# The shift of the router's token rows taken into TensorE as a product of depth 1

## The reference, cut to what matters

```python
h = rms_norm(x, g_ffn) * (1 + scale2) + shift2      # scale2, shift2: one row for context, one for latent tokens
def moe_swiglu(h, w_router, w_gu, w_down):
    t = h.reshape(B * L, D)
    logits = (t @ w_router).astype(jnp.float32)
    top_v, top_i = lax.top_k(logits, TOP_K)
    top_w = jax.nn.softmax(top_v, axis=-1)
    ...                                             # each expert: silu(t @ gate) * (t @ up) @ down, weighted and summed
```

## Time and profile before

| | |
|---|---|
| time, median of 3 executions | 1950.79 us (1949.42 to 1951.01) |
| the profiled execution, its own time | 1948.53 us |
| its span | 1946.7 us |
| PE busy | 1887.4 us (97%) |
| DVE, ACT, POOL busy | 1118.3, 799.6, 139.3 us |

### The profile page before, as it was taken

How to read it: one execution, slowest core, us unless ns; L and a number is a source line. 1 busy time by engine, 2 the same in 40 slices (tenths; PEclk the granted TensorE clock), 3 DMA queues, 4 the chain that set the end, 5 groups by cost and what they waited for, 6 DMA issues and landing times.

```text
span 1946.7 us, 30525 instructions
## 1 busy us (share of the span) xinstructions
PE 1887.4 (97%) x12501; PEld 1726.0 (89%) x12501; DVE 1118.3 (57%) x1796; ACT 799.6 (41%) x1334; POOL 139.3 (7%) x109
## 2 busy tenths in 40 slices
PE   7999989999999999999998899899999999999998
PEld 6999767999999999999997587889898988989896
DVE  2644776544432444447347853667676766768577
ACT  4221264322211222223213643556565655656564
POOL 2000000200000000110000012220000000002211
PEclk8999999999999999999999999999999999999999
DMA  9425100324231432315271031677677676768762
GB/s 353 162 105 217 55 1 23 109 98 183 77 120 44 168 127 74 119 34 195 92 211 34 1 66 61 149 239 243 224 246 226 214 237 203 248 200 304 255 200 76
DMA packets 94068, 291.55 MB, mean 150 GB/s; under 512 B 15348, under 2 KB 23924, under 8 KB 93920
## 3 DMA queue, kind: packets, MB, share of 16 engines
q1 hardware_dynamic: 86784, 271.20, 42.3%
q0 software_dynamic: 7136, 18.30, 2.9%
HBM read 283.02 MB, written 12.28 MB: 152 GB/s over the span
## 4 chain that ended last, share of the span: by engine, by line
PE 90%; DVE 5%; ACT 1%; DMA 1%; issue 1%; SPq 0%; POOL 0%; POOLq 0%; ACTq 0%; DVEq 0%
PE ps L740 47%; PE ps L1119 12%; PE ps L1108 12%; PE ps L1109 6%; PE ps L806 2%; PE ps L935 2%; PE ps L1112 2%; PE ps L881 1%; DVE pr L2037 1%; DVE nbias L2020 1%; PE ps L1111 1%; PE ps L1204 1%; DMA ada_raw<-ada_w 1%; PE ps L942 1%; ACT pT L1448 0%
## 5 line engine op out<-in xcount | busy, mean ns | idle before, releaser
L1867 DVE TENSOR_TENSOR w_lo<-raw,w_hi 128x1024 fp32r<-128x1024 f32 x394 | 482.1, 1225 | 386.0 <-ACT w_hi L1319 377.4
L1319 ACT ACTIVATE w_hi<-raw 128x1024 fp32r<-128x1024 f32 x394 | 414.5, 1053 | 341.7 <-PE ps L740 171.2
L1108 PE MATMUL ps<-hg,w_hi 128*128 128x416 f32 x1232 | 379.2, 365 | 1.0 <-DVE hg L2311 0.8
L740 PE MATMUL ps<-a_hi,w_hi 128*128 128x320 f32 x1472 | 341.9, 313 | 3.4 <-DVE a_lo L1898 3.4
L740 PE MATMUL ps<-a_hi,w_lo 128*128 128x320 f32 x1472 | 336.7, 310 | 0.0
L740 PE MATMUL ps<-a_lo,w_hi 128*128 128x320 f32 x1472 | 333.8, 308 | 0.0
L1109 PE MATMUL ps<-hg,w_lo 128*128 128x208 f32 x1232 | 319.2, 259 | 0.0
L740 PEld LDWEIGHTS ps<-a_hi,w_hi 128*128 128x128 f32 x1472 | 247.4, 188 | 12.1 <-issue 8.1
L740 PEld LDWEIGHTS ps<-a_lo,w_hi 128*128 128x128 f32 x1472 | 248.6, 189 | 0.0
L740 PEld LDWEIGHTS ps<-a_hi,w_lo 128*128 128x128 f32 x1472 | 245.2, 188 | 0.0
L1109 PEld LDWEIGHTS ps<-hg,w_lo 128*128 128x128 f32 x1232 | 234.7, 191 | 0.4
(11 more groups left out here) (285 smaller groups left out, 2446.5 us busy)
## 6 DMA issues: line engine op xcount, KB each, us to landing
raw<-gu_w SPq DMA_DIRECT2D x220, 512.0 KB, 4.4
raw<-moe_down_w SPq DMA_DIRECT2D x88, 512.0 KB, 4.2
ada_raw<-ada_w SPq DMA_DIRECT2D x21, 2048.0 KB, 8.3
raw<-in_w SPq DMA_DIRECT2D x48, 512.0 KB, 9.8
raw<-down_w SPq DMA_DIRECT2D x22, 512.0 KB, 3.4
raw<-out_w SPq DMA_DIRECT2D x16, 512.0 KB, 3.5
ada_pro<-ada_w SPq DMA_DIRECT2D x2, 2048.0 KB, 19.2
y_rows<-ey POOLq DMA_DIRECT2D x7, 512.0 KB, 3.5
```

Of the source, the lines that this page charges most:

```text
L740: ins = nc.tensor.matmul(out[:, hf, 0:c1 - c0], w, o[:, c0:c1], start=f, stop=e)
L1108: nc.tensor.matmul(sums, whi, both, start=(k == 0), stop=False)
L1319: nc.scalar.activation(w_hi[:, s, :], raw[:, n % RAW, :], ACT.Copy).then_inc(hi_done, 1)
L1867: nc.vector.tensor_tensor(w_lo[:, s, :], raw[:, n % RAW, :], w_hi[:, s, :].bitcast(F32), ALU.subtract)\
```

## The change

The row `(x gain) / root + shift` is made as `((x gain) + root shift) / root`. PE turns the five root columns into a row at partition 0 of the norm block, between the fifth and the sixth of the router's eight feature blocks. ACT copies that row to SBUF. `tile_rows` then adds, into the same PSUM block as the turned `hraw`, two fp32 products of depth 1 with 512 columns each: 128 roots by 512 shift values. ACT scales all five blocks out; POOL and DVE add nothing. The shift rows are loaded to partition 0 alone, and the norm block is given back when the root row has been copied. The root is kept in `rms[:, 1, :]`, its reciprocal in `rms[:, 0, :]`. ACT's exponential for the expert weights now comes after all five rows. As a diff, blank lines aside:

```diff
-ROWS_BY_POOL = 3
+        root_row = pr[:].rearrange("p a b c -> p (a b c)")[0:1, 2 * D:2 * D + T]
                     for c in range(2):
-                        sp.dma_start(shift_rows[:, c, :], shifts_d[c].partition_broadcast(P)).then_inc(shift_in, 16)
+                        sp.dma_start(shift_rows[0:1, c, :], shifts_d[c:c + 1, :]).then_inc(shift_in, 16)
                     for t in range(TT):
-                        if t < ROWS_BY_POOL:
-                            sp.wait_ge(ht_pool, t + 1)
-                        else:
-                            sp.wait_ge(ht_dve, t - ROWS_BY_POOL + 1)
+                        sp.wait_ge(ht_scaled, t + 1)
                         sp.dma_start(h_rows[t * P:(t + 1) * P, :], ht[:, t, :]).then_inc(ht_out, 16)
@@ PE, route stage
-                    logits_of(2, KB).then_inc(mm_done, 1)
+                    logits_of(2, KB - 3)
+                    ng = NORM_AT[2 * l + 1][2] % 4
+                    pe.wait_ge(root_done, 2)
+                    for t in range(TT):
+                        at = ps[0:1, ng, 1, t * P:(t + 1) * P] if t < 4 else ps[0:1, ng, 0, P:2 * P]
+                        ins = nc.tensor.transpose(at, rms[:, 1, t:t + 1], idn[:])
+                    ins.then_inc(root_turned, 1)
+                    logits_of(KB - 3, KB).then_inc(mm_done, 1)
                     def tile_rows(b, t):
                         open_block(rg + b)
                         for k in range(KB):
-                            ins = nc.tensor.transpose(ps[:, (rg + b) % 4, k // 4, (k % 4) * P:(k % 4 + 1) * P],
-                                                      hraw[:, k, t * P:(t + 1) * P], idn[:])
+                            nc.tensor.matmul(ps[:, (rg + b) % 4, k // 4, (k % 4) * P:(k % 4 + 1) * P],
+                                             hraw[:, k, t * P:(t + 1) * P], idn[:],
+                                             start=k % 4 == 0, stop=False, is_transpose=True)
+                        if t == 0:
+                            pe.wait_ge(shift_in, 32)
+                            pe.wait_ge(row_ready, 1)
+                        for hf in range(2):
+                            ins = nc.tensor.matmul(ps[:, (rg + b) % 4, hf, 0:512], root_row[:, t * P:(t + 1) * P],
+                                                   shift_rows[0:1, min(t, 1), hf * 512:(hf + 1) * 512],
+                                                   start=False, stop=True)
                         ins.then_inc(mm_done, 1)
@@ ACT
-                nc.scalar.activation(rms[:, 0, :], ps[:, g0 % 4, 0, 0:TT], ACT.Sqrt,
+                nc.scalar.activation(rms[:, 1 if i else 0, :], ps[:, g0 % 4, 0, 0:TT], ACT.Sqrt,
                                      bias=eps[:, 0:1], scale=1.0 / width).then_inc(root_done, 1)
+                    ng = NORM_AT[2 * l + 1][2] % 4
+                    act.wait_ge(root_turned, 1)
+                    nc.scalar.activation(root_row[:, 0:4 * P], ps[0:1, ng, 1, 0:4 * P], ACT.Copy)
+                    nc.scalar.activation(root_row[:, 4 * P:T], ps[0:1, ng, 0, P:2 * P], ACT.Copy).then_inc(row_ready, 1)
                     act.wait_ge(mm_done, rq + 1)
-                    for b, t in ((1, 0), (3, 1), (4, 2)):
+                    for b, t in ((1, 0), (3, 1), (4, 2), (5, 3), (7, 4)):
@@ ACT, before the first x_tok
-                                if i == 0:
-                                    act.wait_ge(ht_pool, ROWS_BY_POOL)
-                                    act.wait_ge(ht_dve, TT - ROWS_BY_POOL)
@@ POOL
-            pool.wait_ge(shift_in, 32)
-            for t in range(ROWS_BY_POOL):
-                pool.wait_ge(ht_scaled, t + 1)
-                nc.gpsimd.tensor_tensor(ht[:, t, :], ht[:, t, :], shift_rows[:, min(t, 1), :], ALU.add)\
-                    .then_inc(ht_pool, 1)
@@ DVE
-                link(nc.vector.reciprocal(rms[:, 0, :], rms[:, 0, :]))
+                link(nc.vector.reciprocal(rms[:, 0, :], rms[:, 1 if i else 0, :]))
                     dve.sem_inc(rms_ready, 1)
+                    dve.wait_ge(row_ready, 1)
                     dve.sem_inc(blk_free, 1)
-                    def shifted_rows(b, t):
-                        ...
-                    shifted_rows(5, 3)
+                    token_rows(3)
-                    shifted_rows(7, 4)
+                    token_rows(4)
```

More of the change, by code:

```diff
@@ L463, in hybrid_step @@
         ht_scaled = sem("ht_scaled")
-        ht_pool = sem("ht_pool")
-        ht_dve = sem("ht_dve")
+        root_turned = sem("root_turned")
+        row_ready = sem("row_ready")
         h_done = sem("h_done")
```

## The result

The change makes the kernel slower: median 1963.77 us (1962.93 to 1965.04, four executions) against 1950.15 (1949.42 to 1951.01) before. The ratio is 1.007, with a 95% interval of 1.0057 to 1.0082, so +13.6 us where the prediction said +0.5. The rival "the clock falls under the products" had 7% and named 1965.

A forecast was written before the change was run, and what follows sets the result against it. PE is busy without a gap from the first product on `hg` at 1237.35, so its start decides. Gather -0.1 to 0 and low part of `hg` 0.4 later gave +0.5, median 1951.3; range 1949 to 1953.5.

The forecast's parts named there:

- the clock falls under the products: Rival: from block 0's products on, one array row may not hold the full clock; +14, 1965, or half, +7; chance 7%.
- The step that failed: PE in the router stage: no idle time from 1196.4 to 1221.8, hence the full clock throughout.
- A product of 512 columns: Shift products on PE: at depth 1 taken as two records 0.43 apart, 0.86, bounded between 0.43 and 1.72.
- the cheap product: Rival: a depth-1 product in `tile_rows` is one record, 0.43; about -3.5, 1947.3; chance 4%.
- The stalls of 1.4 and 2.0: Two DVE operations during POOL's additions lose 3.4 in all, swallowed because the mask then waits for PE until 1215.55.
- The last rows and the gather: End of the token rows: last store issued within 0.1 of before; gather starts at 1224.8 and lands at 1233.1.
- the 4.85 from rows to gather: Time from the end of the last token rows to the landing of their store, kept from before.
- DVE's low part of `hg`: Just before the first expert: released by `places`, not ACT, and starting 0.4 later, with ±0.3 for rounding.
- The block of `tile_rows`, 2.58: PE per token block: eight turns at 0.108 plus two products, 1.72, make 2.58.
- The third chain: `idx`, ACT's copies of x, `places`, low part of `hg`: `idx` ends 1.55 later, `places` starts 1.2 later, 0.4 remains on the path.

The follow-up runs named there:

- depth 64: The changed kernel with the depth of the shift products raised from 1 to 64 by equal root and shift rows; 1953.54 us, run once.
- depth-32 kernel: The changed kernel with the depth of the shift products raised from 1 to 32; 1966.22 us, ratio 1.0086 against the kernel before.
- depth-128 twin: The changed kernel with 128 equal root rows, scaled by 1/128, and 128 equal shift rows; 1951.04 us, ratio 1.0009 against the kernel before.
- idle products of depth 128: The kernel before with two unused fp32 products of depth 128 ahead of each token block's turns; 1949.69 us, ratio 1.0004.
- the kernel with `places` early: The changed kernel at depth 128 with `places` ahead of DVE's wait for the first copy of x; 1952.51 us, ratio 1.0013.
- reordered pair: Roots-on-a-diagonal kernel, count before the fourth token block, two filler groups removed, `places` early: 1949.76 us; with SP waiting for gathered rows before weight loads: 1946.81 us.
- late loads: SP waits for the gathered rows before issuing weight loads behind its branch; 1951.83 us in the changed kernel at depth 128, 1947.72 in the kernel before.
- the diagonal: The changed kernel with roots on a 128x128 diagonal times 128 equal shift rows, without root turns and row copies; 1950.8 us, ratio 1.0004.

## Why the prediction was wrong, step by step

**The step that failed is "The new timeline has no idle PE from 1196.4 to 1221.8, so I take the full clock throughout".** It took idleness for the only cause of a fall, because the one fall before the branch in the trace of before came with a wait. PE was indeed never idle, and the clock fell at about 1207.5. In place of that step the runs show that a mix with products of depth 1 or 32 loses the clock and that depth 64 and 128 keep it, in the changed kernel and, at depths 1 and 128, in the kernel before. The rival with 7% had named this fall; the forecast did not follow it, for no row spoke either way. The Trainium skill ("TensorE: Matmul & The Clock Gate", section "Why this matters for your kernels") says that a single matmul with a depth of 32 takes as long as one with 128. Block 0 of the depth-32 kernel agrees at the full clock (0.43 per record), but the rule leaves out what the kernel pays for afterwards, and it would have given the forecast's +0.5.

**The rival's size.** It said that the work from 1204.4 to 1218.55 doubles, +14. The kernel after and its depth-128 twin differ by 11.6 in the stage, because the fall came 3.1 later than block 0's first product. Of that difference the estimate above gives 1.4 to the switches between depths. Behind the stage comes the second fall, 1.6. The medians give 12.7 between the two.

**What was right**, read from the depth-128 kernel, in which the failed step holds:

- A product of 512 columns is two records 0.43 apart at depths 1, 32, 64 and 128, at the full clock. Neither one record (the cheap product, 4%) nor more.
- POOL's additions had held up DVE. The stalls of 1.4 and 2.0 went, and the gain was swallowed, for the mask was done at 1211.12 and PE counted from 1214.85. Where the idle products of depth 128 shifted POOL's additions, the stalls moved with them.
- The last rows and the gather hardly move at the full clock and depth 128. The rows are ready 24.0 behind the stage's start, where it had been 23.6, and the gather starts at 27.85, where it had been 28.49. The two differ because the 4.85 from rows to gather, which the working kept, was 3.88; why is not shown.
- DVE's low part of `hg` is released by `places`.

**What was mis-sized.** The block of `tile_rows`, 2.58, holds at depth 128 alone; at depth 64, the lowest that kept the clock, it is 2.94. There the gather starts 29.3 behind the stage's start, so even at the full clock the change would have moved it by some 0.8 (an estimate, with depth 64 in place of depth 1). The third chain was given +0.4. In the depth-128 kernel the first product comes 2.1 later than before, counted from the stage's start. Its `places` starts 3.0 later and not 1.2: PE's `idx` comes 2.0 later and not 1.55, and PE's fifth turn of x waits 2.07 for DVE behind its branch, which the working did not have at all, and ACT's last copy of x waits with it. Of these 2.1 the medians show 1.0; starts of the stage alone spread from 1194.5 to 1197.0 between single profiles, so one profile can't place the last microsecond. The last expert's 1.6, if it belongs to the change, would be part of it too. Together that is a matter of 1 to 2 us, inside the range of the forecast; the miss came from the clock.

**What stays open.** How long DVE needs across its branch: 7.58 in the kernel with `places` early, 5.08 and 4.94 in the reordered pair without and with the late loads, and, by the start of the fifth turn, 7.5 at depth 128 and 8.3 at depth 64. In the depth-128 kernel the late loads let its fifth turn of x start at 1229.84 instead of 1231.16, but in the reordered pair they changed this gap by 0.14 only, so traffic alone doesn't account for it. Nor is it shown why the products behind a wait of 2 to 3 us, at the first expert and in the last one, sometimes run at half clock and sometimes not.

## What to carry to other kernels

A product's price is its own time and what it does to the clock of everything around it. Before a small matmul is put into a stage that is bound by TensorE, give it many rows, by operands repeated over the rows or spread out as on the diagonal (rows of zeros in both operands were not tried): at the same number of columns these cost nothing measurable here, and they kept 12 us, most of it by the clock. "PE is busy" in a window says nothing of the clock; read the granted clock beside it, and where no row shows the new shape's effect on it, give that case a chance to match the ignorance.

## What the runs showed of the hardware

- At granted clock 0.50 for 20 us PE was busy in every microsecond; in the kernel with idle products of depth 128 it idled 1.5 in 18 and kept 1.00. A stationary operand with 127 zeros in 128 held the clock as a full one did.
- A weight load ran under the product before it when both had depth 128 (at 1208.34), and not when the product had depth 64; a block of eight turns and two products took 2.60 and 2.94.
- While POOL added 128x1024 values in SBUF, a cast of 40 columns, two subtractions of 5 and an addition of 40 ended with POOL's instruction and took up to 2.25 instead of 0.2, while the MAX8 of 8 columns beside it kept its 0.17. The stall moved to other instructions when POOL's additions moved.
- A gather took longer with transfers issued beside it: 8.35 between its issue and its reader, and 6.49 once they were held back (9.66 and 6.63 in the reordered pair), with 2.2 us less of median in an otherwise unchanged kernel (ratio 0.9988).
